# Branch A's queries and keys from two seven-product quads ahead of the heads, with the transfers of the weight sums issued by GpSimd

## The reference

```python
h = _rmsnorm(x, norm_g[l])
proj = jnp.einsum('bsd,df->bsf', h, w_in[l])        # 512 x 2048 by 2048 x 20480
aq, ak, av, az = parts[0:4]                         # branch A: 8 heads of 2 x 64
b_qkv = parts[4:4 + 3 * n_g]                        # branch B: 3 groups, 8 heads of 128
bz = parts[4 + 3 * n_g]
cb, cc, cx, cz = parts[5 + 3 * n_g:9 + 3 * n_g]     # branch C: gated convolution
gates = jax.nn.sigmoid(parts[9 + 3 * n_g] + gate_b[l]).reshape(bsz, seq, N_BRANCH, D_MODEL)
...
oa = _diff_attention(aq, ak, av, lam, slopes_a)     # p = softmax_0 - lam * softmax_1, causal
oa = (_rmsnorm(oa, subln_g[l]) * (1.0 - lam_init)).reshape(bsz, seq, A_WIDTH)
ya = oa * jax.nn.silu(az)
...                                                 # yb, yc, then per-branch projections,
...                                                 # merge by the gates, output projection,
return _rmsnorm(x, final_g)                         # residual and final norm
```

## Time and profile before

| | |
|---|---|
| runs | 2529.17, 2530.38, 2530.74 us |
| median | 2530.38 us |
| profiled execution | 2530.92 us |
| its span in the trace | 2529.1 us |
| TensorE busy | 2501.1 us (99%), 11486 matmuls and transposes |
| VectorE busy | 1963.6 us (78%) |
| ScalarE busy | 1031.8 us (41%) |
| GpSimd busy | 0.2 us |
| granted TensorE clock | 0.999 of full speed |
| DMA | 501.98 MB, mean 198 GB/s |

### The profile page before, as it was taken

How to read it: one execution, slowest core, us unless ns; L and a number is a source line. 1 busy time by engine, 2 the same in 40 slices (tenths; PEclk the granted TensorE clock), 3 DMA queues, 4 the chain that set the end, 5 groups by cost and what they waited for, 6 DMA issues and landing times.

```text
span 2529.1 us, 30668 instructions
## 1 busy us (share of the span) xinstructions
PE 2501.1 (99%) x11486; PEld 2065.3 (82%) x11486; DVE 1963.6 (78%) x2294; ACT 1031.8 (41%) x1273; POOL 0.2 (0%) x4
## 2 busy tenths in 40 slices
PE   9999999999999999999999999999999999999998
PEld 8888888888888888888887788888878887788787
DVE  8797746767676767676768887789878897898875
ACT  5343323233333233333244433344444445655644
POOL 0000000000000000000000000000000000000000
PEclk9999999999999999999999999999999999999999
DMA  8255255566665566665235545545566455787665
GB/s 315 96 193 191 78 193 196 187 237 221 237 220 204 188 237 221 237 220 204 81 111 189 211 167 191 174 158 181 186 222 202 165 174 201 275 284 243 216 229 202
DMA packets 172709, 501.98 MB, mean 198 GB/s; under 512 B 13585, under 2 KB 50706, under 8 KB 169362
## 3 DMA queue, kind: packets, MB, share of 16 engines
q1 hardware_dynamic: 88448, 338.44, 38.7%
q10 hardware_dynamic: 84114, 161.56, 18.1%
HBM read 407.67 MB, written 92.27 MB: 198 GB/s over the span
## 4 chain that ended last, share of the span: by engine, by line
PE 89%; DVE 5%; DMA 4%; issue 1%; ACT 1%; ACTq 0%; SPq 0%; DVEq 0%
PE proj L600 14%; PE proj L602 14%; PE proj L601 14%; PE sc_ps L600 6%; PE sc_ps L602 6%; PE sc_ps L601 6%; PE tr_ps L600 5%; PE tr_ps L602 5%; PE tr_ps L601 5%; PE o_ps L600 3%; PE o_ps L602 3%; PE o_ps L601 3%; DVE w_lo L1459 2%; DMA raw<-s_dram 1%; DMA rows<-c_dram 1%; PE tr_ps L637 1%
## 5 line engine op out<-in xcount | busy, mean ns | idle before, releaser
L600 PE MATMUL proj<-act_hi,w_hi 128*128 128x512 f32 x1280 | 505.4, 395 | 1.2 <-DVE w_lo L1503 1.2
L602 PE MATMUL proj<-act_hi,w_lo 128*128 128x512 f32 x1280 | 499.1, 390 | 0.0
L601 PE MATMUL proj<-act_lo,w_hi 128*128 128x512 f32 x1280 | 498.4, 389 | 0.0
L971 ACT ACTIVATE w_hi<-raw 128x1024 fp32r<-128x1024 f32 x280 | 296.9, 1060 | 409.6 <-PE proj L602 127.9
L1459 DVE TENSOR_TENSOR w_lo<-raw,w_hi 128x1024 fp32r<-128x1024 f32 x280 | 341.4, 1222 | 148.5 <-ACT w_hi L971 147.8
L971 ACT ACTIVATE w_hi<-kb 128x1024 fp32r<-128x1024 f32 x240 | 254.4, 1061 | 371.9 <-PE proj L602 133.6
L1459 DVE TENSOR_TENSOR w_lo<-kb,w_hi 128x1024 fp32r<-128x1024 f32 x240 | 293.3, 1223 | 96.3 <-ACT w_hi L971 95.5
L1503 DVE TENSOR_TENSOR w_lo<-raw,w_hi 128x1024 fp32r<-128x1024 f32 x160 | 195.7, 1223 | 128.3 <-ACT w_hi L1012 125.8
L602 PEld LDWEIGHTS proj<-act_hi,w_lo 128*128 128x128 f32 x1280 | 240.3, 188 | 51.1
L600 PEld LDWEIGHTS proj<-act_hi,w_hi 128*128 128x128 f32 x1280 | 240.9, 188 | 49.4 <-DVE w_lo L1503 1.4
L601 PEld LDWEIGHTS proj<-act_lo,w_hi 128*128 128x128 f32 x1280 | 240.6, 188 | 48.0
(11 more groups left out here) (318 smaller groups left out, 4551.4 us busy)
## 6 DMA issues: line engine op xcount, KB each, us to landing
raw<-wst SPq DMA_DIRECT2D x160, 512.0 KB, 4.2
raw<-wg SPq DMA_DIRECT2D x112, 512.0 KB, 4.0
kb<-wg SPq DMA_DIRECT2D x24, 2048.0 KB, 8.0
ssum<-ws ACTq DMA_DIRECT2D x24, 2048.0 KB, 9.4
s_dram<-ssum ACTq DMA_DIRECT2D x24, 2048.0 KB, 7.7
raw<-s_dram SPq DMA_DIRECT2D x96, 512.0 KB, 4.3
raw<-ws SPq DMA_DIRECT2D x72, 512.0 KB, 4.3
kb<-wg SPq DMA_DIRECT2D x48, 512.0 KB, 6.8
```

What stands on the lines that cost most here:

```text
L600: nc.tensor.matmul(out, w_h, a_h, start=first, stop=False, skip_group_check=shared)
L601: nc.tensor.matmul(out, w_h, a_l, start=False, stop=False, skip_group_check=shared)
L602: return nc.tensor.matmul(out, w_l, a_h, start=False, stop=last, skip_group_check=shared)
L971: nc.scalar.activation(w_hi[r % RING][:, :], src, ACT.Copy).then_inc(hi_done, 1)
```

## The change

**Projection of `aq` and `ak`.** Two quads more (`QUADS_V` 4 to 6) compute the queries and keys of branch A for all heads; they stand second and third, behind the plain one. The heads keep eight blocks, Q0 to BZ, or 16 units (`NHU1` 20 to 16). For each head ACT loads its 128 columns of both (`load_qa`, two tiles of 128 x 4 x 128), one head ahead. PE turns them by four transposes each (`turn_block`), AQ between the two units of Q0 and AK between those of K0; ACT makes the high part from the PSUM bank (`high_turn`) and DVE the low part (`low_turn`).

**Work that moves with it.** w now starts at 2 (Q0). `scores_a(q)` stands in blocks w = 4 to 7, `values_a` at the end of w = 9. The sum of squares, its root and the divisor move into the next head (`squares_a(i - 1)` in block Q0 behind the transposes of AQ, `root_o` and the tanh of BZ in w = 2, `inverse_a` in w = 4). In the last head `values_a`, `probs_b(0)` and `scores_b(1)` stand between the two units of BZ, and the squares, the root (with its table loads) and `inverse_a` are in the first quad after the heads.

**Weight sums.** GpSimd issues all loads and stores of `ssum` in a loop of its own, from the eighth unit of the last quad before the heads: load, wait for the adds, store, wait for the store, next load. The adds stay on DVE; in the heads they stand behind `split(t)` for t = 2, 6, 10, 14 in head 0, t = 2, 7, 11 in the loop's k = 1, t = 0, 4, 9, 14 in k = 2 and t = 2, 7, 11 in k = 3.

```diff
-NBLK1, NHU1 = 10, 20
+NBLK1, NHU1 = 10, 16
+ENTRY = {AQ: 0, Q0: 1, AK: 2, K0: 3} | {b: b for b in range(Q1, NBLK1)}
-QUADS_V, QUADS_C, QUADS_G, QUADS_O = 4, 8, 14, 2
+QUADS_V, QUADS_C, QUADS_G, QUADS_O = 6, 10, 16, 2
+Q_AQ, Q_V = 1, 3
-SUMS_AT = {0: (5, 10), 1: (0, 5, 10, 15), 2: (0, 5, 10, 15), 3: (0, 5, 10), HEADS - 1: ()}
-SUMS_LOOP = 11
+SUM_AT = 2
+SUMS_FIRST = (0, 4, 8, 12)
+SUMS_LOOP = (0, 5, 9, 14, 18, 23, 28, 32, 37, 41)
...
+            def turn_block(h, b):
+                i, bank = h.i, pb[h.bank(b)]
+                pe.wait_ge(qa_in[b], 16 * i + 16)
+                pe.wait_ge(evac_done, NBLK1 * i + (ENTRY[b] + 1))
+                for n in range(4):
+                    end = nc.tensor.transpose(bank[:, n * P:(n + 1) * P], qa[b][:, n, :], ident[:, :])
+                end.then_inc(a_turned, 1)
...
+                for w in range(Q0, NBLK1):
+                    t = 2 * (w - Q0)
...
+                    multiply(h.bank(w), h.slot(t), act_hi, act_lo, 0, True, False)
+                    if w == Q0:
...
+                        turn_block(h, AQ)
+                        if not fresh:
+                            squares_a(i - 1)
+                    if w == K0:
+                        turn_block(h, AK)
+                    if last and w == 9:
+                        values_a(i)
+                        probs_b(i, 0)
+                        scores_b(i, 1, True)
...
+                    if w < 4 and not fresh:
+                        scores_b(i - 1, w)
+                    if w < 5 and not fresh:
+                        probs_b(i - 1, w - 1)
...
+                    if 4 <= w < 8:
+                        scores_a(i, w - 4)
+                    if 5 <= w < 9:
+                        probs_a(i, w - 5)
...
-                    m = h.sums(t, LOAD_AT)
-                    if m is not None:
-                        act.wait_ge(osum_stored, 16 * m + 16)
-                        act.dma_start(ssum[:, :, :], ws[bass.ds(m, 1), :, :, :].rearrange("o t p q -> p (o t) q")).then_inc(osum_in, 16)
-                    m = h.sums(t, SAVE_AT)
...
+            def high_turn(h, b):
+                act.wait_ge(a_turned, 2 * h.i + (TURNED.index(b) + 1))
+                nc.scalar.activation(qk_hi[b][:, :], pb[h.bank(b)][:, :], ACT.Copy).then_inc(a_hi, 1)
...
+                    if w == 2 and not fresh:
+                        act.wait_ge(s_free, 9 * i - 9 + (6 + SQ_AFTER))
+                        root_o(i - 1)
+                        tanh_half(i - 1, BZ)
...
                     if q == QUADS_V:
                         if n == 3:
+                            act.wait_ge(last_read, 1)
+                            root_o(HEADS - 1)
                             turned_b(HEADS - 1, 1)
                         if n == 4:
                             exps_b(HEADS - 1, 3)
+                            tanh_half(HEADS - 1, BZ)
...
+        @block.gpsimd
+        def _(pool):
+            pool.wait_ge(pe_used, RING + first_unit(QUADS_V - 1) + 2 * NU)
+            for m in range(SUMMED):
+                if m:
+                    pool.wait_ge(osum_stored, 16 * m)
+                pool.dma_start(ssum[:, :, :], ws[m, :, :, :].rearrange("t p q -> p t q")).then_inc(osum_in, 16)
+                pool.wait_ge(osum_done, m + 1)
+                pool.dma_start(s_dram[m, :, :, :].rearrange("t p q -> p t q"), ssum[:, :, :]).then_inc(osum_stored, 16)
...
+            def low_turn(h, b):
+                dve.wait_ge(a_hi, 2 * h.i + (TURNED.index(b) + 1))
+                tt(qk_lo[b][:, :], pb[h.bank(b)][:, :], qk_hi[b][:, :].bitcast(f32), ALU.subtract).then_inc(evac_done, 1)
...
+                    split(t)
+                    if w == Q0:
+                        low_turn(h, AQ)
...
                     if w == 2 and not fresh:
+                        dve.wait_ge(s_ready, 9 * i - 9 + (5 + SQ_AFTER))
+                        ts(sq_a[:, :], sc_ps[0][:, :], 1.0 / P, EPS, ALU.mult, ALU.add).then_inc(s_free, 1)
+                    if w == 4 and not fresh:
                         low_v(2 * i, v_b)
                         inverse_a(i - 1)
...
                         else:
+                            copy_o(i)
                             bias_b(i, 1)
                             turned_b(i, 0)
+                            low_squares(i)
...
                         if n == 3:
+                            dve.wait_ge(last_sq, 1)
+                            ts(sq_a[:, :], pb[0][:, :], 1.0 / P, EPS, ALU.mult, ALU.add).then_inc(last_read, 1)
                             turned_b(HEADS - 1, 1)
                             norm_b(HEADS - 1, 2)
-                            bias_b(HEADS - 1, 3)
+                            bias_b(HEADS - 1, 3, True)
+                        if n == 6:
+                            inverse_a(HEADS - 1)
```

More of the change, by code:

```diff
@@ L175, in gated, with step_b @@
     return 8 * q + 2 * GATED.index(d) + s + 1
-SPLIT = [AQ, AK, Q0, K0]
+SPLIT = [Q0, K0]
+TURNED = [AQ, AK]
+SQ_AFTER = 2
+def step_b(c, last):
+    return 5 + c + (not last and c >= SQ_AFTER)
 TURN_P = [4, 6, 8, 10]
@@ L1118, in head @@
                             store_y(i - 1, 0, y_a)
-                    if w == 5:
+                    if w == 7:
                         if not fresh:
@@ L1142, in head @@
-                    if w == 8:
-                        act.wait_ge(s_free, 9 * i + 6)
-                        nc.scalar.activation(inv_a[:, :], sq_a[:, :], ACT.Sqrt).then_inc(sd_ready, 1)
+                    if w == 3 and not fresh:
+                        act.wait_ge(vb_in, 16 * i)
+                        act.wait_ge(o_ready, 2 * i - 1)
+                        high_v(v_b)
+                    if w < 4 and not fresh:
+                        exps_b(i - 1, w)
+                    if w == 3:
+                        for b in SPLIT:
+                            split_block(i, b)
@@ L1149, in head @@
                         exps_b(i, w - 8)
-                    if w == 9:
+                    if last and w == 9:
                         act.wait_ge(vb_in, 16 * i + 16)
@@ L1229, in _ @@
                     end_of(q, n)
+                    if q == QUADS_V - 1 and n == 16:
+                        for m in range(8):
+                            act.wait_ge(g_stored[m], 16 * Q_V)
+                        load_qa(0)
                     if q == QUADS_V - 1 and n == 23:
@@ L1722, in head @@
                 link(nc.vector.tensor_copy(slope[:, 0:1], slopes[:, bass.ds(4 * i, 1)]))
[L1723 to L1726 removed]
+                for w in range(Q0, NBLK1):
+                    t = 2 * (w - Q0)
+                    if w < 5 and not fresh:
+                        norm_b(i - 1, w - 1)
+                    if fresh and w == 5:
                         for n in range(8):
                             dve.wait_ge(g_stored[n], 16 * QUADS_V)
[L1729 to L1730 removed]
+                    if 5 <= w < 9:
+                        norm_a(i, w - 5)
                     if w == 9:
                         norm_b(i, 0)
[L1733 removed]
+                    split(t)
+                    if w == Q0:
+                        low_turn(h, AQ)
+                    if w == K0:
+                        low_turn(h, AK)
                     if last:
```

264 lines of the change are left out of this document (125 added, 139 removed).

## The result

The changed kernel takes 2536.16 us (median of 20 runs), the kernel before 2529.45 on the same chips: 1.0028 of it, 95% interval 1.0022 to 1.0035. It is slower by 0.28% where I had forecast no change; the 14.7 us that TensorE saves are there, and 21 us are given back.

The account below looks back on a forecast made before the run. The prediction took TensorE, busy 2501.1 of 2529.1 us, as the bound. From 2530.92 us profiled, -14.7 (matmuls), +10.7 (waits in heads) and +3 (behind the last head) gave 2529.9, or 2529.5 as a median; range 2520 to 2541.

Parts of the forecast that it names:

- no change: Whole kernel: the saving is given back in waits, 2525.3 to 2535.4 us, likeliest 2529.5; chance 0.48.
- Matmuls removed and added: TensorE's own work: 174.1 us off in the heads, 152.4 on for two quads, 7.0 for transposes; net -14.7 us.
- New waits in the heads: Heads: PE waits for work queued behind 4.8 us sums at four new places; +10.7 us, taken as 2 to 18.
- t = 11: Block K2, k = 1 and 3: the sum delays `pr` of query block 3; 1.1 us four times, 4.4 us.
- t = 0: Block Q0, k = 2: the sum delays the scaling of the squares that PE needs; 2.0 us twice, 4.0 us.
- t = 14: Block BZ: the sum and DVE and ACT passes behind it end after PE arrives; 0.5 us three times, 1.5 us.
- Transfers by GpSimd: `ssum` round trips, 17.6 us, at most 22.6, against gaps of about 19 to 28 us: costed at nothing.
- case C: Heads: GpSimd's transfers each 3 us later than ACT's, DVE stands before sums; +11 us, 2541 us, slower; chance 0.13.
- The rule that I had weighed: GpSimd's DMA descriptors cannot be written during VectorE's two-port fast operations; case C's time if all VectorE work delayed transfers.
- Behind the last head: First quad after the heads: root on ACT and `inverse_a` on DVE come, the `z_b` wait goes; +3 us, bounds -1.9 to +5.3.
- case D: Quad behind the heads loses its rhythm, PE waits for `w_lo`, window over 92 us; 2537 to 2543 us, slower; chance 0.13.
- the later loads from `s_dram` take up some lateness: Quad behind the heads: these loads, 9.88 us in the chain, absorb some lateness; one reason for taking +3 us.

Follow-up runs that it names:

- e5: Changed kernel with each sum's adds working on only 8 of 1024 columns, transfers and order kept: 2516.21 us, 0.9942 of before.
- e2: Changed kernel, same table of sums, but ACT instead of GpSimd issues the transfers of `ssum`: 2534.57 us, 1.0007 of before.
- e3: Kernel before the change with only the issuing of `ssum` loads and stores moved to GpSimd, adds five units apart: 2531.74 us, 1.0006 of before.
- e4: Changed kernel; behind the heads, ACT copies turned probabilities ahead of the root, and `inverse_a`'s reciprocal is made in halves: 2534.52 us, 1.0017 of before.
- e1: Changed kernel, loop sums moved to t = 2, 7, 12 (k = 1, 3) and 1, 5, 9, 14 (k = 2): 2536.56 us, 1.0024 of before.
- e7: Changed kernel with the table of e6 (t = 2, 7, 12; k = 2: 1, 6, 10, 14), but ACT issues the transfers: 2520.31 us, 0.9964 of before.
- e10: e6 with GpSimd's first load of the loop's second turn held until PE finishes that turn's first unit: 2529.08 us, 0.9996 of before.
- e6: Changed kernel, GpSimd issuing, loop sums at t = 2, 7, 12 (k = 1, 3) and 1, 6, 10, 14 (k = 2): 2536.26 us, 1.0022 of before.
- e11: Changed kernel, GpSimd issuing, loop sums at t = 2, 7, 12, two halved sums in the last quad, e10's wait, e4's edits: 2534.84 us, 1.0016 of before.

## Why the prediction was wrong

- **"Matmuls removed and added", -14.7 us:** right. The two quads put off the start of head 0 by 151.7 us (152.4 forecast), loop heads take 105.37 without sums (105.3), and PE is busy 2485.2 us in e5 (2486).
- **"New waits in the heads", +10.7:** t = 11 1.05 each (1.1 forecast), t = 0 2.04 (2.0), t = 14 in the loop 0.5 (0.5), t = 9 nothing (0.4): 9.3 us in the changed kernel. The term came out at 19.2: 4.2 at the squares and 0.6 for `pr` behind late sums of head 0, 3.2 by the clock (both next), and some 1.9 in pieces that I did not follow up. Of the 4.2, 0.5 was forecast, for t = 14 of head 0.
- **"Transfers by GpSimd ... I cost this at nothing":** this is the step that failed. I took "store and load of the next 17.6" against "in head 0 about 19", a cover of 1.4 us, from medians of transfers issued by ACT, and then spoke of a cover of 3.7, which holds in the loop. GpSimd's store and load took 18.7 to 21.3 with what lies between them; lateness adds up over four sums in a row, and falls on the squares. Part of this isn't GpSimd's: ACT's took 19.4 and 19.6 in the same head (e2). I had held against case C that the heads load less weight, but head 0 now has four sums in 98 us where it had two in 119, and its DMA share went from 0.52 to 0.71. Case C had the mechanism, but wanted 3 us per transfer. e2 takes the lateness away by the issuer and comes out at 1.0007 of before, no change, as forecast: 3.3 us at the squares, 0.6 at `pr` and 1.6 of clock go, about the 5 us between the ratios. e3 takes it away by the gap of five units (there are fewer sums in the same time as well; the two weren't separated). The rule that I had weighed (the Trainium skill, "SBUF — State Buffer", section "SBUF: two separate sides", descriptors held up while VectorE is in a two-port mode) is not shown to be at work: GpSimd's own instruction takes 0.74 to 0.88 us in all 48 cases, and by the profile page the load takes 10.5 us to land where ACT's takes 9.3 in e2, the store 8.1 for 7.4, while in the kernel before the two issuers are within 0.2 of each other (e3). The advice of the Trainium skill in that section, to issue from ACT, was nevertheless right for this kernel by 5 us with one table and 16 with the other; its reason isn't shown here.
- **The clock.** No term was there for it. It fell to half behind the wait of 4.2 us and behind one of the two of 2.04: 1.6 + 1.6 = 3.2 us in the profiled execution.
- **"Behind the last head", +3:** +4.4 (-0.7 and +5.1), within the bounds given. Both culprits were named, the root on ACT (1.5 us at the quad's fifth unit, whose `w_lo` came 0.1 before PE took it) and `inverse_a` (2.1 at its eighth; case D looked for just such a wait for `w_lo`, with a window over 92, and so it came, though D's own terms make 2538 to 2540 and not up to 2543); "the later loads from `s_dram` take up some lateness" did not come true, and e4 gets back 2.3 us of the window by placing alone.

By size: 8.5 us too little in the heads and 1.4 behind them, less 2.5 us elsewhere, is the difference between my sum of -1 and the +6.4 of the traces. The forecast's range (2520 to 2541) held the time; "no change", whose band ended at 2535.4, did not.

The claim that the places of the sums are what costs was first contradicted by e1 and then borne out by e2 against e7, where the issuer is the same and only the table differs: 1.0007 and 0.9964, 11 us. With GpSimd the same step of the table brings nothing (1.0028 to 1.0022), since its own lateness and the turn of the loop take the place of the waits removed; with the load held over the turn (e10) it brings 8 us, to 0.9996. The table pays in full only with ACT as issuer.

## What to carry to other kernels

When a change shortens a stage, what rides along in it (here 24 sums, each a load, four adds and a store) keeps its length: work out the round trip of a single buffer against the new distance with the slow transfers, stage by stage, and ask what the last sum in a row is ahead of. A loop that issues transfers as early as it can is not the same as one that issues them at chosen units: early transfers can fall on the turn of a hardware loop (e6) or on a stretch whose DMA engines are full (e11). And where a table places filler work, list first what stands behind each place within the cover of the ring; a table changed by guesswork trades one wait for another.

## What the runs showed that I had not expected

- PE's wait at the turn of this hardware loop is 1.2 to 1.7 us, and 4.6 and 3.9 in the two traces in which a 2 MB load of GpSimd is under way at that moment (e1 and e6); holding the load back takes it to 1.3 (e10).
- After a wait of 4.2 us TensorE was granted half its clock for some 3.5 us, beginning a microsecond after it resumed, in the middle of a row of matmuls. The twelve traces with the change show how regular this is, from head 0 to the quad behind the heads: behind each of the ten longest waits (3.4 to 8.3 us) the clock fell, at 1.4 to 3.0 us each; behind 13 of the 24 waits of 2.0 to 2.7 us, mostly at 1.7 us; and behind none of those of 1.0 to 1.9 us that began at the full clock. So one and the same wait of 2.04 us costs 2.0 us or 3.7.
- A 2 MB load took 17.4 us across the end of a quad, where the DMA engines were full, and 10.7 by the median in the heads (e11).
